# Second mixer of a two-block network: lengths of query and key heads by one product with ones for two heads

## The reference, cut to what matters

```python
GDN_HEADS, GDN_DK, GDN_DV, GDN_CONV = 8, 128, 128, 4

def l2norm(x):
    return x * lax.rsqrt(jnp.sum(x * x, axis=-1, keepdims=True) + 1e-6)

def gated_deltanet(qkv, z, beta_logit, a_logit, conv_w, a_log, dt_bias, norm_w, w_o):
    qkv = jax.nn.silu(causal_dwconv(qkv, conv_w))
    q, k, v = jnp.split(qkv.astype(jnp.float32), [W_Q, W_Q + W_K], axis=-1)
    q = l2norm(q.reshape(b, l, GDN_HEADS, GDN_DK)) * (GDN_DK ** -0.5)
    k = l2norm(k.reshape(b, l, GDN_HEADS, GDN_DK))
    ...

h = rmsnorm_2(x, mix_norm_pre[i])
p = h @ mix_w_in[i]
qkv, z, beta_logit, a_logit, glu_in, gates = jnp.split(p, SPLITS, axis=-1)
y_a = gated_deltanet(qkv, z, beta_logit, a_logit, ...)
y_b = conformer_conv(glu_in, ...)
y = (g_a * y_a + g_b * y_b) @ mix_w_out[i]
x = x + rmsnorm_2(y, mix_norm_post[i])
```

## Time and profile before

| | us |
|---|---|
| median of 3 runs | 2831.6 |
| lowest and highest | 2831.0, 2835.13 |
| the profiled execution's own time | 2832.48 |
| its span in the profile | 2830.7 |

### The profile page before, as it was taken

One profiled execution on the slowest core, in us unless ns is written; L12 is line 12 of the kernel. 1 busy time (PEld: TensorE's weight loads), 2 busy tenths in 40 slices (PEclk: granted clock), 3 DMA queues, 4 the chain that ended last, 5 costly groups with the idle time before them and its releaser, 6 DMA issues.

```text
span 2830.7 us, 46605 instructions
## 1 busy us (share of the span) xinstructions
PE 2733.8 (97%) x17368; PEld 2360.3 (83%) x17368; DVE 1580.8 (56%) x2439; ACT 1463.0 (52%) x2136; POOL 899.4 (32%) x469
## 2 busy tenths in 40 slices
PE   7999999999999999999989999999999899999999
PEld 6888897887878997878879899878778798998787
DVE  5543854545544844545546585655455466756554
ACT  5445565445445655445455644654454556446543
POOL 0007563001017666010028554720100285547200
PEclk9999999999999999999999999999999999999999
DMA  5555445655555446556558542456555585424664
GB/s 183 184 182 153 132 138 178 186 186 176 185 167 156 132 142 193 186 172 191 184 137 201 113 91 73 148 183 186 176 182 185 139 197 120 91 69 149 186 186 142
DMA packets 368426, 450.01 MB, mean 159 GB/s; under 512 B 32510, under 2 KB 266112, under 8 KB 368224
## 3 DMA queue, kind: packets, MB, share of 16 engines
q1 hardware_dynamic: 366896, 446.34, 53.6%
q10 hardware_dynamic: 400, 0.43, 0.1%
q0 software_dynamic: 928, 0.45, 0.1%
HBM read 446.06 MB, written 1.05 MB: 158 GB/s over the span
## 4 chain that ended last, share of the span: by engine, by line
PE 87%; DVE 5%; ACT 4%; POOL 2%; issue 1%; DMA 0%; ACTq 0%; DVEq 0%
PE PS L505 26%; PE PS L507 25%; PE PS L506 25%; POOL wl L541 2%; PE PS L661 1%; ACT wh L533 1%; ACT xh L1279 1%; DVE PS L2078 1%; DVE wl L541 1%; PE PS L1072 1%; PE PS L770 1%; PE PS L1007 1%; PE PS L1139 1%; PE PS L638 1%; PE PS L998 1%
## 5 line engine op out<-in xcount | busy, mean ns | idle before, releaser
L541 POOL TENSOR_TENSOR wl<-ring,wh 128x1024 fp32r<-128x1024 f32 (+1 forms) x348 | 835.9, 2421 | 1728.5 <-ACT wh L533 1727.4
L533 ACT ACTIVATE wh<-ring 128x1024 fp32r<-128x1024 f32 x848 | 890.4, 1055 | 919.2 <-PE PS L505 880.4
L541 DVE TENSOR_TENSOR wl<-ring,wh 128x1024 fp32r<-128x1024 f32 x500 | 611.8, 1225 | 630.8 <-ACT wh L533 630.7
L505 PE MATMUL PS<-wh,xh 128*128 128x512 f32 x1600 | 634.0, 396 | 33.2 <-DVE xl L1782 25.3
L507 PE MATMUL PS<-wh,xl 128*128 128x512 f32 x1600 | 623.2, 390 | 0.0
L506 PE MATMUL PS<-wl,xh 128*128 128x512 f32 x1600 | 622.1, 389 | 0.0
L505 PE MATMUL PS<-xh,wh 128*128 128x256 f32 x1888 | 554.4, 294 | 1.7 <-DVE xl L1782 1.7
L506 PE MATMUL PS<-xl,wh 128*128 128x256 f32 x1888 | 539.3, 286 | 0.0
L507 PE MATMUL PS<-xh,wl 128*128 128x256 f32 x1888 | 538.9, 285 | 0.0
L505 PEld LDWEIGHTS PS<-wh,xh 128*128 128x128 f32 x1600 | 301.2, 188 | 101.5 <-issue 34.9
L505 PEld LDWEIGHTS PS<-xh,wh 128*128 128x128 f32 x1888 | 367.0, 194 | 22.5 <-issue 16.2
(11 more groups left out here) (296 smaller groups left out, 2604.6 us busy)
## 6 DMA issues: line engine op xcount, KB each, us to landing
ring<-in_ffn_w_in_dram SPq DMA_DIRECT2D x352, 256.0 KB, 3.0
ring<-in_mix_w_in_dram SPq DMA_DIRECT2D x256, 256.0 KB, 3.8
ring<-in_w_in_dram SPq DMA_DIRECT2D x200, 256.0 KB, 3.0
ring<-in_ffn_w_gate_dram SPq DMA_DIRECT2D x176, 256.0 KB, 2.9
ring<-in_ffn_w_up_dram SPq DMA_DIRECT2D x176, 256.0 KB, 3.1
ring<-in_ffn_w_down_dram SPq DMA_DIRECT2D x176, 256.0 KB, 2.7
ring<-in_ffn_w_out_dram SPq DMA_DIRECT2D x176, 256.0 KB, 2.7
ring<-in_w_branch_dram SPq DMA_DIRECT2D x32, 256.0 KB, 2.9
```

The lines of the kernel that those rows point to most:

```text
L505: first_ = mm(o, w[0], x[0], start=start, stop=False, skip_group_check=True)
L533: act_(dst, src, ACT.Copy).then_inc(hi_ready, 1)
L541: (engine or v_).tensor_tensor(dst, src, part_views(t, wh)[0], ALU.subtract).then_inc(lo[t.slot()], 1)
```

## The change

The lengths are now made for a pair of heads at a time. One product of ones (128x128) with the squares of two heads (512 columns) gives the sums on all 128 partitions, so that no spreading is needed. ScalarE takes Ln and Exp of the whole bank (128x512) in place, and VectorE's `unit` follows ScalarE. The first pair's product stands after tile 0, the second's after tile 1, and the second waits for the first pair's `unit`, as both use bank 4. ScalarE makes one conversion between the two roots and one behind them, with a table load ahead of the first and one after the last conversion of the three. VectorE's short convolution is cut in two: the first pair's `unit` stands between the halves, the second pair's after the second half and two steps of the long convolution. `pick` and its two setup instructions are gone.

```diff
--- before.py
+++ after.py
@@ -222,7 +222,6 @@
         levels, tmask = masks[:, 0:7 * P].rearrange("p (l n) -> p l n", l=7), masks[:, 7 * P:8 * P]
         cmask, cosT, sinT = (masks[:, i * S:(i + 1) * S] for i in range(3))
         ones64, rot = masks[:, 6 * P:7 * P], masks[:, 7 * P:8 * P]
-        pick = sb("pick", [7])
         W = sb("W", [WIDE])
         PS = ctx.enter_context(nc.psum_tensor("PS", [P, 8, 512], F32))
 
@@ -988,25 +987,16 @@
                         ins = nc.tensor.transpose(bank(4, 16 * j + 8 * c, 16 * j + 8 * c + 8), src, ident[0:8, 0:8])
                 ins.then_inc(m2[0].sem, m2[0].did("tok"))
 
-            def sums(n):
+            def sums(j):
+
+                n = j // 2
                 pe.wait_ge(m2[1].sem, m2[1].at(f"l2sq{n}"))
-                if n == 0:
+                if j == 0:
                     pe.wait_ge(m2[1].sem, m2[1].at("btok"))
                 else:
-                    pe.wait_ge(m2[2].sem, m2[2].at(f"l2n{2 * n - 1}"))
-                for h in range(4):
-                    ins = mm(PS[0:4, 4, 0:S], pick[:, 3 - h:7 - h], sq[:, 4 * (n % 2) + h, :], start=(h == 0), stop=(h == 3))
-                ins.then_inc(m2[0].sem, m2[0].did(f"l2s{n}"))
-
-            def spread(j):
-                pe.wait_ge(m2[1].sem, m2[1].at(f"l2.{j // 2}.rstd"))
-                if j % 2 == 1:
                     pe.wait_ge(m2[2].sem, m2[2].at(f"l2n{j - 1}"))
-                for i in range(2):
-                    h = 2 * (j % 2) + i
-                    ins = mm(bank(4, i * S, (i + 1) * S), ident[0:4, h:h + 1].to_broadcast([4, P]), rstd[0:4, 0, 0:S],
-                             start=True, stop=True)
-                ins.then_inc(m2[0].sem, m2[0].did(f"l2b{j}"))
+                mm(bank(4), ones, sqp(2 * (n % 2) + j % 2), start=True, stop=True).then_inc(
+                    m2[0].sem, m2[0].did(f"l2s{j}"))
             pe_small2(pe, t, "BETA", 4, s)
             pe_small2(pe, t, "A", 5, s)
             group("GLU_G0", 2)
@@ -1022,7 +1012,7 @@
             group("QKV1", 0)
             for n in range(2, 6):
                 pe.wait_ge(m2[1].sem, m2[1].at(f"cp.QKV{n - 2}"))
-                group(f"QKV{n}", (n + 1) % 2 * 2, {0: lambda: sums(n - 2), 2: lambda: spread(2 * n - 4), 3: lambda: spread(2 * n - 3)})
+                group(f"QKV{n}", (n + 1) % 2 * 2, {0: lambda: sums(2 * n - 4), 1: lambda: sums(2 * n - 3)})
             pe_delta(pe, t)
 
             def ready_a(c):
@@ -1497,25 +1487,21 @@
 
             def square(n):
                 if n >= 2:
-                    e.wait_ge(m2[0].sem, m2[0].at(f"l2s{n - 2}"))
+                    e.wait_ge(m2[0].sem, m2[0].at(f"l2s{2 * n - 3}"))
                 e.wait_ge(m2[1].sem, m2[1].at(f"silu{n}"))
                 act_(sq[:, n % 2 * 4:n % 2 * 4 + 4, :], heads[:, 4 * n:4 * n + 4, :], ACT.Square).then_inc(
                     m2[1].sem, m2[1].did(f"l2sq{n}"))
 
-            def root(n):
-                e.wait_ge(m2[0].sem, m2[0].at(f"l2s{n}"))
-                if n:
-                    e.wait_ge(m2[0].sem, m2[0].at(f"l2b{2 * n - 1}"))
-                tables(LN_EXP)
-                r_ = rstd[0:4, 0, 0:S]
-                act_(r_, PS[0:4, 4, 0:S], ACT.Ln, bias=consts[0:4, 0:1]).then_inc(m2[1].sem, m2[1].did(f"l2.{n}.ln"))
-                e.wait_ge(m2[1].sem, m2[1].at(f"l2.{n}.ln"))
-                if n < 2:
-                    ins = act_(r_, r_, ACT.Exp, scale=-0.5, bias=consts[0:4, 3:4])
+            def root(j):
+
+                e.wait_ge(m2[0].sem, m2[0].at(f"l2s{j}"))
+                act_(bank(4), bank(4), ACT.Ln, bias=consts[:, 0:1]).then_inc(m2[1].sem, m2[1].did(f"l2.{j}.ln"))
+                e.wait_ge(m2[1].sem, m2[1].at(f"l2.{j}.ln"))
+                if j < 4:
+                    ins = act_(bank(4), bank(4), ACT.Exp, scale=-0.5, bias=consts[:, 3:4])
                 else:
-                    ins = act_(r_, r_, ACT.Exp, scale=-0.5)
-                ins.then_inc(m2[1].sem, m2[1].did(f"l2.{n}.rstd"))
-                tables(SILU_TANH)
+                    ins = act_(bank(4), bank(4), ACT.Exp, scale=-0.5)
+                ins.then_inc(m2[1].sem, m2[1].did(f"l2.{j}.rstd"))
 
             def gated(num):
                 e.wait_ge(m2[0].sem, m2[0].at(f"p.GLU_G{num}"))
@@ -1546,8 +1532,14 @@
             for n in range(6):
                 high(e, t, 1)
                 if n >= 2:
-                    root(n - 2)
-                high(e, t, 2)
+                    tables(LN_EXP)
+                    root(2 * n - 4)
+                high(e, t, 1)
+                if n >= 2:
+                    root(2 * n - 3)
+                high(e, t, 1)
+                if n >= 2:
+                    tables(SILU_TANH)
                 if n:
                     silu(n - 1)
                     if n <= 4:
@@ -2018,9 +2010,6 @@
             v_.memset(consts[:, 0:1], EPS)
             v_.memset(consts[:, 2:3], math.log(0.5))
             v_.memset(consts[:, 3:4], -0.5 * math.log(P))
-            v_.memset(pick, 0.0).then_inc(pro_dve.sem, pro_dve.did("pick0"))
-            e.wait_ge(pro_dve.sem, pro_dve.at("pick0"))
-            v_.memset(pick[:, 3:4], 1.0)
             v_.memset(consts[:, 1:2], LN_EPS).then_inc(pro_dve.sem, pro_dve.did("consts"))
             e.wait_ge(pos_in, 16)
             v_.tensor_copy(posf, pos_i).then_inc(pro_dve.sem, pro_dve.did("posf"))
@@ -2095,9 +2084,9 @@
                                                 env.g2[:, 4 * num + b, B_A:B_A + 1], gth[:, b, :], ALU.add,
                                                 ALU.mult), f"glu.{num}.{b}")
 
-            def short(n):
+            def short(n, b0s=(0, 2)):
                 e.wait_ge(m2[1].sem, m2[1].at(f"cp.QKV{n}"))
-                for b0 in (0, 2):
+                for b0 in b0s:
                     for tap in range(CTAPS):
                         for b in (b0, b0 + 1):
                             r = W_CV + 3 * tap + n // 2
@@ -2115,7 +2104,7 @@
                             did(ins, f"q.{n}.{tap}.{b}")
 
             def unit(j):
-                e.wait_ge(m2[0].sem, m2[0].at(f"l2b{j}"))
+                e.wait_ge(m2[1].sem, m2[1].at(f"l2.{j}.rstd"))
                 z = blk2(heads, j)
                 did(v_.tensor_tensor(z, z, bank(4), ALU.mult), f"l2n{j}")
             did(v_.memset(glu[:, :, 0:TAPS - 1], 0.0), "pad0")
@@ -2138,9 +2127,11 @@
             e.wait_ge(m2[1].sem, m2[1].at("btok"))
             step(e, m2, v_.tensor_tensor(bgtok, bgtok, btok, ALU.mult), "bgtok")
             for n in range(6):
-                short(n)
+                short(n, (0,))
                 if 1 <= n <= 4:
                     unit(2 * n - 2)
+                short(n, (2,))
+                if 1 <= n <= 4:
                     taps(2)
                     unit(2 * n - 1)
                     taps(3)
```

## The result

| | before | changed |
|---|---|---|
| median, us | 2832.06 (4 runs) | 2810.99 (4 runs) |
| lowest and highest | 2831.0, 2835.13 | 2808.68, 2811.33 |
| profiled execution, its span | 2832.48, 2830.7 | 2808.68, 2806.9 |

The ratio is 0.9922, 95% interval 0.9905 to 0.9939: 21 us or 0.8% faster. The forecast was 2814.2, with a range of 2809.5 to 2823.

A forecast was written before the change was run, and what follows sets the result against it. TensorE was taken as the bound: 2.1 us saved in each of eight rounds (16.8) plus 0.6 after the stage, 17.4 off 2832.5, gives 2815.1, or 2814.2 us as a median 0.9 lower. Range 2809.5 to 2823.

The forecast's parts named there:

- What bounds it: Whole kernel, above all the QKV projection stage: TensorE, busy in 97% of the span, sets the time; other engines are cover.
- The removed products: TensorE, QKV2 to QKV5 rounds: one-column sums and four-row spreads, 3.9 us, plus breaks, 4.5 us a round removed.
- each of the three interruptions: TensorE between tile products in a round: each break costs 0.19 us beyond its small products, 0.57 together.
- The added products: TensorE, each round: two 512-column products with ones at 1.0 us, plus two breaks, 2.4 us; 2.1 saved per round.
- The new waits: Second sum of a round waits for VectorE's first-pair product: slack 0.9 us, 0.6 with ScalarE late by 0.2; nothing charged.
- signs of being wrong: Next profile: TensorE idles before second sums, a round over 14.5 us, or the stage's granted clock under 1.00.
- After the stage: First delta-rule broadcasts: second layer's TensorE wait goes, first layer's clock uncertain; +0.6 us saved, bounds -1.5 to +2.5.
- Rival A: Second sums wait: each round loses 0.5 to 1.2 us, 4 to 10 us less gain, 2818 to 2824; chance 0.14.
- Rival B: ScalarE becomes the bound at 15.3 us a round, as with 1.38 us drain per table switch; 2826.5; chance 0.04.
- Rival C: New waits in the rounds pull TensorE's clock down, 1.7 us each; slower, 2840 at waits of 1.5; chance 0.05.
- threshold of w = 0.4: Wait per round from which wait plus 1.7 us of slow clock outweighs the 2.1 us saved.
- Rival D: QKV stage isn't shortened: weights' transfers or ScalarE set the pace; 2826 to 2832; chance 0.05.

The follow-up runs named there:

- the doubled sum: Changed kernel with each product with ones made twice; 2820.45 us in its one time.
- wide sums and wide spreads: Kernel before, with 128-column weight blocks for the sums, and roots and spreads on 128 rows instead of 4; 2829.36 us, ratio 0.9988 to before.
- wide sums: Kernel before, with each head's sum made by a weight block of 128 columns instead of 4, spreads still 4 rows; 2830.53 us, ratio 0.9999 to before.
- two halves: Changed kernel with each 512-column product with ones cut into two of 256 columns; 2811.49 us in its one time.
- four rows: Changed kernel whose sums take only the first 4 of 128 rows, still 512 columns, Ln scale set to 1000; 2824.01 us in its one time.
- convolution whole: Changed kernel with VectorE's short convolution whole again, ahead of the first scaling of a pair; median 2833.63 us, ratio 1.0006 to before.
- one pass: Changed kernel with squares and ones in the one-pass format of the tile products; median 2807.62 us.
- one pass, squares on VectorE: Changed kernel with one-pass squares and ones, squares made by VectorE, ScalarE's first conversion moved behind the first root; median 2800.32 us, ratio 0.9894 to before.
- table load behind the wait: Changed kernel with a round's first table load behind the wait for the first sum, as before the change; 2819.49 us in its one time.
- first conversion behind the first root: Changed kernel with ScalarE's first conversion of a round moved behind the first root; 2808.02 us, ratio 0.9918 to before.

## Why the prediction was right, point by point

The time lies 3.2 us under the forecast and 1.5 inside the fast end of the range. The mechanism was right, one term of the sum was too small, and the number profits from a range that was wide for other reasons. The stage alone saved 21.3 us, where the forecast's bounds for it were 16.0 to 17.6.

- **What bounds it.** Right: TensorE, unbroken. Shown by the doubled sum, 0.85 per product, and by the waits of two experiments, which cost themselves and, in one of them, two falls of the clock.
- **The removed products** at 4.5 us a round: right as a sum, 16.00 less 11.52. But its 0.57 for "each of the three interruptions" was read as a price of interrupting. It is the price of thin products, and they cost more than that: in the kernel with wide sums and wide spreads the same eight products of 256 columns leave a round of 14.95, so thinness took 1.05, which is 0.28 at the sums and 0.39 at each pair of spreads. The part that is missing in the 0.57 the prediction had counted as the length of the thin products themselves.
- **The added products** at 2.4 us a round: this term was mis-sized. It measured 1.7, two times 0.85. I had taken the pair of four-row spreads as an upper bound (1.0 rather than 0.86) and charged two breaks that a wide product doesn't have. The earlier trace rows already showed two wide products at a spacing of 0.43 per record. Saved per round: 2.8 instead of 2.1. The two stages together lost 21.3 instead of 16.8, 4.5 more than forecast, and the median lies 3.2 below the forecast.
- **The new waits.** Right in mechanism, too large in slack: 0.6 was forecast from the second round on, but it was next to nothing in the second round and less than nothing in the third, where TensorE waits 0.23. Two readings took the slack away. The prediction let the next tile begin when the sum's last record ends, so TensorE would ask 4.05 after the first sum's start; it asks at 3.73. In-place Ln is 0.66, Exp 0.66 with a bias and 0.58 without, inside 1.2 to 1.5. And ScalarE's lateness is 0.46, 0.80 and 0.44 in the first layer's last three rounds for the 0.2 I had. Of the signs of being wrong, one stood in this one round (TensorE idles before a second sum); the rounds stayed under 14.5 and the clock at 1.00.
- **After the stage.** Forecast 0.6, bounds -1.5 to +2.5; the delta rule's stage was 3.6 and 2.8 shorter in the two profiles of the changed kernel, outside the bounds. The wait in the second layer is gone as forecast (7.92 us between the broadcasts for 8.45). In the first layer the clock did not fall behind the first broadcasts (7.92 for 9.30), but it fell behind the second ones. The medians show less of it: 21.1 and 20.7 us in all, no more than the stage's own 21.3. The length of the delta rule's stage goes mostly by how often TensorE runs at the 1.2 GHz level in it, in stretches that cost 1 to 2 us each (18 tile products at 0.21 instead of 0.12 are 1.7):

| kernel | delta rule's stage, both layers, us | stretches at 1.2 GHz |
|---|---|---|
| before | 237.3, 236.6 | 4, 3 |
| wide sums | 236.6, 237.5 | 3, 4 |
| wide sums and spreads | 237.7, 238.9 | 4, 5 |
| changed, two profiles | 235.5, 234.8; 235.5, 235.6 | 3, 3; 3, 3 |
| two halves | 237.2, 235.7 | 4, 3 |
| four rows | 239.5, 239.3 | 5, 5 |
| convolution whole | 237.0, 236.8 | 3, 4 |
| one pass | 235.8, 238.3 | 3, 5 |
| one pass, squares on VectorE | 235.8, 237.2 | 3, 4 |

A stretch of double length is counted twice. The three kernels that are not listed (table load behind the wait, each sum twice, first conversion behind the first root) have three stretches in each layer and 235.1 to 235.7. The two layers of the kernel with sums in one pass, the clock third from the end:

```profile
1601.90:1837.70 235.80, 225.65 (x2474) 212.69 (x2473) 151.23 (x297) 119.91 (x196) 134.26 (x72) 0.98 0.40 109
2366.60:2604.90 238.30, 228.24 (x2474) 215.37 (x2474) 156.42 (x297) 119.95 (x196) 134.11 (x72) 0.96 0.38 107
```

With three stretches each, the changed kernel is about 1 us a layer below the kernels before it (234.8 to 235.6 for 236.6), of which the waits behind the stage explain 0.9 (0.57 gone, and the next one 0.5 instead of 0.8). The first layer's 1.8 in the profiles is one stretch less, and the kernel with two halves did not have that.
- **Rival A** (waits) took 0.2 us. **Rival B**'s drain is not there: a load behind its wait cost 0.6 to 0.7 us a round as 1.28 alone would. ScalarE is close to being the bound all the same: at 12.9 us a round it is, as the sums in one pass show. **Rival C** did not occur, but it exists: the waits of the whole convolution brought the clock down twice a layer, after 2.8 or 2.5 us and after 1.8. Its price of 1.7 for a fall was right. Its threshold of w = 0.4 asked for a fall in each round, and that never came: waits of 0.7 in every round left the clock at 1.00, and so did the first two of 1.6 and 2.5. **Rival D** fell: 10 to 11 us per layer came through to the end.

Open: what decides how often the clock falls in the delta rule's stage. It differs between the two layers of one execution (3 and 5 with the sums in one pass), where TensorE leaves the same 2474 records in both. The most falls follow thin sums (5 and 5 with four rows), but wide ones have 5 too. No run tells whether the products before it or its place in time decide.

## What to carry to other kernels

Count a small product on a TensorE-bound path by its columns and its format (512 columns are 0.85 us in fp32 and 0.23 in the one-pass format here), and keep it as wide as its neighbours: letting one product of ones write the sum to all 128 partitions makes summing and spreading one step. A stage with everything hidden has its next bound close by, so find out what the other engines' rounds take before cutting further. Here the reordering that came with it, the convolution cut in two, was worth as much as the whole gain: without it TensorE waits about 9 us a layer, the clock falls, and the time is back where it was. A difference of a few us outside the changed stage needs more than one profile before it is put down to the change.

## What was not expected of the hardware

- A fp32 product with 4 rows costs 0.39 us more than one with 128 rows and the same 512 columns when it stands between full ones: 0.09 ahead of it and 0.30 behind. With 4 columns of weights and all rows it is 0.28 for a group of four products (the sums before against the wide sums).
- Both are in line with a rule of the Trainium skill ("TensorEngine Tiling (Array Packing)", Tiling Modes) that a change of tiling mode drains TensorE; whether thin products run in another mode no row here names.
- The one-pass format takes a quarter of fp32's time for 512 columns (0.23 against 0.85), though fp32 shows two records and it one.
- Waits of TensorE of 1.6 and 2.5 us in 16 us rounds left the granted clock at 1.00; after the third, of 2.8 in one layer and 2.5 in the other, it was at 1.2 GHz, and again after the fourth, of 1.8. So the length of one wait alone does not decide.
- Whole-kernel times of single runs missed what the changed stage explains by 7 us one way and 4 the other (thin rows +7, doubled sum -4). With thin rows the four more stretches at the lower clock in the delta rule, at 1.7 each, are about that much. With effects under 5 us the stage's rows told more than the median.
